# A Trainium2 kernel of two transformer stacks: half of two output chunks ahead of the heads' norm, the fourth chunk ahead of the third, both token blocks scaled in a row

## The reference, cut to what matters

```python
def _retention_diff_mixer(...):        # layer 0
    ret = _merge(_group_norm(_bidirectional_scan(q, k, v, la_f, la_b))) * jax.nn.silu(rg)
    diff = _merge(_rms_norm(o, subln) * (1.0 - lam_init))
    return jnp.concatenate([ret, diff], axis=-1) @ w_out
def _mla_gla_mixer(...):               # layer 1
    gla = _merge(_rms_norm(o, gla_norm)) * jax.nn.silu(gg)
    return jnp.concatenate([mla, gla], axis=-1) @ w_out
# first block, each layer
x = _layer_norm(ALPHA * x + mix, ln1_g[i], ln1_b[i])
x = _layer_norm(ALPHA * x + _hier_moe(x, ...), ln2_g[i], ln2_b[i])   # 32 experts, 2 of them for a token
# second block, each layer: feed-forward, mixer, feed-forward
y_hgrn = head_rms_norm(o, hgrn_norm_g[l]) * jax.nn.silu(g)
mix = jnp.concatenate([y_pool, y_hgrn], axis=-1) @ w_out[l]
x = layer_norm(ALPHA_2 * x + mix, ln_g[l, 1], ln_b[l, 1])
```

## Time and profile before

| | |
|---|---|
| time, median of 3 runs | 2363.29 us (2363.08 to 2366.67) |
| the profiled execution | 2362.22 us, its span 2360.2 us |
| PE busy | 2174.5 us, 92% |
| DVE busy | 1143.2 us, 48% |
| ACT busy | 785.6 us, 33% |
| DMA, mean over the span | 264 GB/s (420 GB/s while the experts run) |
| last products of the mixers' ends | 176.9, 829.0, 1637.9 and 2159.9 us |

### The profile page before, as it was taken

The page is one execution under the profiler, slowest core; times in us unless marked ns, Lnnn a source line. Parts: engine busy times, 40 slices in busy tenths (PEclk is TensorE's granted clock), DMA queues, the critical chain, the costliest instruction groups (busy, mean ns, idle before and its releaser), DMA issues.

```text
span 2360.2 us, 30107 instructions
## 1 busy us (share of the span) xinstructions
PE 2174.5 (92%) x12126; PEld 1535.9 (65%) x12126; DVE 1143.2 (48%) x1782; ACT 785.6 (33%) x1299; POOL 60.4 (3%) x62
## 2 busy tenths in 40 slices
PE   8978998799887889997988999998999999898998
PEld 7874443344367844433433688897888888787887
DVE  5563221121157741211211766676666666776666
ACT  3432110011035321101111455453554555544553
POOL 0010000000010000000000000001000000001000
PEclk9989999899998799999999999999999999999999
DMA  9438999999972289999999855533555555433551
GB/s 292 142 119 360 420 420 421 417 421 421 417 251 72 70 351 420 420 421 415 421 420 420 287 178 202 173 126 114 187 181 197 176 181 198 159 107 125 179 195 56
DMA packets 231542, 622.66 MB, mean 264 GB/s; under 512 B 15456, under 2 KB 166944, under 8 KB 182112
## 3 DMA queue, kind: packets, MB, share of 16 engines
q1 hardware_dynamic: 226096, 605.32, 67.8%
q0 software_dynamic: 3040, 10.78, 1.4%
q10 hardware_dynamic: 2256, 4.50, 0.5%
HBM read 619.51 MB, written 1.05 MB: 263 GB/s over the span
## 4 chain that ended last, share of the span: by engine, by line
PE 41%; DMA 6%; DVE 4%; ACT 2%; issue 1%; SPq 0%; POOL 0%; DVEq 0%; ACTq 0%
PE bank L1507 14%; PE bank L1495 9%; PE bank L1508 7%; PE bank L228 6%; PE bank L1335 3%; DMA arena<-in_moe_w_up 1%; DMA ring<-in_moe_w_up 1%; DMA w_parts<-in_moe_w_up 1%; DMA ring<-in_ffn_gate 1%; DMA x_tok<-in_moe_w_up 1%; DVE w_low L429 1%; PE bank L1663 1%; ACT w_high L422 0%; DVE x_tok L683 0%; DVE x_tok L672 0%
## 5 line engine op out<-in xcount | busy, mean ns | idle before, releaser
L429 DVE TENSOR_TENSOR w_low<-ring,w_high 128x1024 fp32r<-128x1024 f32 x364 | 440.6, 1225 | 270.2 <-ACT w_high L422 270.1
L1507 PE MATMUL bank<-xT_parts,w_high 128*128 128x512 f32 x1408 | 497.8, 396 | 6.0 <-DVE xT_parts L494 6.0
L422 ACT ACTIVATE w_high<-ring 128x1024 fp32r<-128x1024 f32 x364 | 376.9, 1053 | 217.2 <-PE bank L1508 185.6
L1508 PE MATMUL bank<-xT_parts,w_low 128*128 128x256 f32 x1408 | 395.4, 281 | 0.0
L1335 PE MATMUL bank<-ring,arena 128*64 128x512 f32 x1344 | 339.5, 594 | 18.0 <-DMA ring<-in_moe_w_up 5.9
L1507 PEld LDWEIGHTS bank<-xT_parts,w_high 128*128 128x128 f32 x1408 | 264.7, 188 | 69.1 <-DVE xT_parts L494 6.9
L1335 PE MATMUL bank<-w_parts,arena 128*64 128x512 f32 x768 | 262.1, 604 | 12.4 <-DMA w_parts<-in_moe_w_up 5.7
L1508 PEld LDWEIGHTS bank<-xT_parts,w_low 128*128 128x128 f32 x1408 | 266.8, 189 | 3.0
L1335 PEld LDWEIGHTS bank<-ring,arena 128*64 128x64 f32 x1344 | 110.0, 137 | 231.7 <-issue 222.9
L228 PE MATMUL bank<-w_high,xT_parts 128*128 128x256 f32 x1152 | 229.2, 296 | 14.0 <-DVE w_low L429 8.8
L1443 DVE SCALAR_TENSOR_TENSOR arena<-arena,bank 128x512 f32<-128x512 f32 x32 | 23.9, 748 | 435.3 <-PE bank L1335 435.3
(11 more groups left out here) (285 smaller groups left out, 2930.5 us busy)
## 6 DMA issues: line engine op xcount, KB each, us to landing
ring<-in_moe_w_gate SPq DMA_DIRECT2D x56, 1024.0 KB, 24.1
ring<-in_moe_w_up SPq DMA_DIRECT2D x56, 1024.0 KB, 22.1
ring<-in_moe_w_down SPq DMA_DIRECT2D x56, 1024.0 KB, 26.1
ring<-in_ffn_gate SPq DMA_DIRECT2D x44, 1024.0 KB, 6.9
ring<-in_ffn_up SPq DMA_DIRECT2D x44, 1024.0 KB, 5.4
ring<-in_ffn_down SPq DMA_DIRECT2D x44, 1024.0 KB, 6.4
w_parts<-in_moe_w_up SPq DMA_DIRECT2D x32, 1024.0 KB, 26.3
w_parts<-in_moe_w_down SPq DMA_DIRECT2D x32, 1024.0 KB, 26.1
```

Source lines behind the costliest of these rows:

```text
L422: e.activation(hi, src, ACT.Copy).then_inc(*S.high.tell(key))
L429: e.tensor_tensor(lo, src, hi.bitcast(F32), ALU.subtract).then_inc(*S.low.tell(key))
L1507: e.matmul(pairs(bank[:, :]), hi[:, j, :], k.x_parts[:, :, j, :], start=j == 0, stop=False)
L1508: ins = e.matmul(bank[:, 0:T], lo[:, j, :], k.xh[:, j, :], start=False, stop=j == KT - 1)
```

## The change

It does four things, in all four ends:

1. `begin_out_pe` makes the ready half of chunks 0 and 1 (48 products) ahead of the transposes; 144 are left for `out_pe`. Chunk 1 gets a bank for each block.
2. The order of `out_pe` becomes (0,0), (1,0), (0,1), (1,1), (3,0), (2,0), (3,1), (2,1).
3. ScalarE copies the high parts of chunks 1 and 3 before the squares (or, in the even layer, before the mix); VectorE makes chunk 1's low parts ahead of the norm and chunk 3's beside it. What the fourth chunk's copies wait for is now the last reader of that part of the arena (`arena_free`): the last retention scores, the last level's scores, or the last decayed level. In the even layer `b.dq, b.dk, b.rq, b.rk` move to the arena's end.
4. Both blocks are scaled and gated in a row; block 0's mix low part comes after them.

```diff
--- before.py
+++ after.py
@@ -404,6 +404,15 @@
     return src, hi[i][:, :].rearrange("p (a b) -> p a b", a=a), lo[i][:, :].rearrange("p (a b) -> p a b", a=a)
 
 
+def arena_free(k, name, layer):
+
+    if name == "ev_out":
+        return k.S.product, ("ret", 3)
+    if name == "od_out":
+        return k.S.product, k.od.streams[1].last(1)
+    return k.S.dve_step, ("hgrn", layer, 1, "decayed", 1)
+
+
...
     old = k.part_before[key]
     if key[0] in ("ev_out", "od_out", "out2") and key[2] == 3:
-        e.wait_ge(*S.used[key[0:2] + (0, 1)])
+        signal, last = arena_free(k, key[0], key[1])
+        e.wait_ge(*signal[last])
     if old is not None:
         e.wait_ge(*(S.expert[old] if old[0] == "moe" else S.used[old]))
     e.activation(hi, src, ACT.Copy).then_inc(*S.high.tell(key))
@@ -578,48 +588,52 @@
 
 
 
-def begin_out_pe(e, k, name, layer, r, rest):
-
-    S = k.S
-    key = (name, layer, 0)
-    e.wait_ge(*S.low[key + (1,)])
+def begin_out_pe(e, k, name, layer, r, rest, group):
+
+    S = k.S
     for mix in rest:
         e.wait_ge(*S.dve_out[mix])
-    _, hi, lo = split_views(k, key + (r,))
-    for tb in range(NB):
-        bank = k.banks.open(e, B_BANKS, key + ("tb", tb))
-        mm(e, bank[:, 0:256], block_products(k, tb, hi, lo, r * (KT // 2)), last=False)
+    for c in range(2):
+        key = (name, layer, c)
+        e.wait_ge(*S.low[key + (1,)])
+        _, hi, lo = split_views(k, key + (r,))
+        for tb in range(NB):
+            bank = k.banks.open(e, group if c else B_BANKS, key + ("tb", tb))
+            mm(e, bank[:, 0:256], block_products(k, tb, hi, lo, r * (KT // 2)), last=False)
 
 
 def out_pe(e, k, name, layer, r, mixes):
 
     S = k.S
-    for c, tb in ((0, 0), (0, 1), (1, 0), (1, 1), (2, 0), (3, 0), (2, 1), (3, 1)):
+    for tb in range(NB):
+        e.wait_ge(*S.dve_out[mixes[tb]])
+        for c in range(2):
+            key = (name, layer, c)
+            _, hi, lo = split_views(k, key + (1 - r,))
+            ins = mm(e, k.banks[key + ("tb", tb)][:, 0:256], block_products(k, tb, hi, lo, (1 - r) * (KT // 2)), first=False)
+            ins.then_inc(*(S.used.tell(key + (1,)) if tb == 1 else S.product.tell(key + ("tb", 0))))
+    for c, tb in ((3, 0), (2, 0), (3, 1), (2, 1)):
         key = (name, layer, c)
-        if c == 0:
-            bank, c0 = k.banks[key + ("tb", tb)], 0
-        elif c == 1:
-            bank, c0 = k.banks.open(e, A_BANKS, key) if tb == 0 else k.banks[key], tb * 256
-        else:
-            bank, c0 = k.banks.open(e, A_BANKS if c == 2 else B_BANKS, key + ("tb", tb)), 0
+        bank = k.banks.open(e, A_BANKS if c == 2 else B_BANKS, key + ("tb", tb))
         e.wait_ge(*S.low[key + (1,)])
-        e.wait_ge(*S.dve_out[mixes[tb]])
         parts = []
-        for part in (1 - r,) if c == 0 else (0, 1):
+        for part in (0, 1):
             _, hi, lo = split_views(k, key + (part,))
             parts += block_products(k, tb, hi, lo, part * (KT // 2))
-        ins = mm(e, bank[:, c0:c0 + 256], parts, first=c > 0)
-        if tb == 1:
-            ins.then_inc(*S.used.tell(key + (1,)))
-        elif c != 1:
-            ins.then_inc(*S.product.tell(key + ("tb", 0)))
+        ins = mm(e, bank[:, 0:256], parts)
+        ins.then_inc(*(S.used.tell(key + (1,)) if tb == 1 else S.product.tell(key + ("tb", 0))))
+
+
+def out_ahead_act(e, k, name, layer):
+
+    split_chunk(e, k, (name, layer, 1), split_act)
+    split_chunk(e, k, (name, layer, 3), split_act)
 
 
 def out_act(e, k, name, layer):
-    for c in range(4):
-        split_chunk(e, k, following(k, (name, layer, c)), split_act)
-        if c == 2 and name != "out2":
-            split_act(e, k, ("router", 0 if name == "ev_out" else 1))
+    split_chunk(e, k, (name, layer, 2), split_act)
+    if name != "out2":
+        split_act(e, k, ("router", 0 if name == "ev_out" else 1))
 
 
 def residual_dve(e, k, key, blocks, cols, src):
@@ -628,25 +642,18 @@
 
 
 def out_dve(e, k, name, layer, norm):
-    S = k.S
-    for c in range(4):
-        key, cols = (name, layer, c), slice(256 * c, 256 * c + 256)
-        split_chunk(e, k, following(k, key), split_dve)
-        if c == 0:
...
-        if c == 2 and name != "out2":
-            split_dve(e, k, ("router", 0 if name == "ev_out" else 1))
-
-
-def out_last_dve(e, k, name, layer, c, tb):
+    for tb in range(NB):
+        out_residual_dve(e, k, name, layer, 0, tb)
+    split_chunk(e, k, (name, layer, 2), split_dve)
+    for tb in range(NB):
+        out_residual_dve(e, k, name, layer, 1, tb)
+        e.wait_ge(*k.S.dve_out[name, layer, 1, "tb", tb])
+        half_stats(e, k, norm, tb, 0)
+    if name != "out2":
+        split_dve(e, k, ("router", 0 if name == "ev_out" else 1))
+
+
+def out_residual_dve(e, k, name, layer, c, tb):
 
     S = k.S
     key, cols = (name, layer, c), slice(256 * c, 256 * c + 256)
...
@@ -884,7 +891,7 @@
         elif what == "mix":
             for tb in range(NB):
                 mix_transposes_pe(e, k, k.acc[:, :, 512:1024], tb, ("diff_mix", tb), ("diff_o", NB - 1))
-    begin_out_pe(e, k, "ev_out", 0, 1, [("diff_mix", 1)])
+    begin_out_pe(e, k, "ev_out", 0, 1, [("diff_mix", 1)], O_BANKS)
     for tb in range(NB):
         mix_transposes_pe(e, k, k.acc, tb, ("ret_mix", tb), ("ret_y", tb))
     out_pe(e, k, "ev_out", 0, 1, [("ret_mix", 0), ("ret_mix", 1)])
...
+    out_ahead_act(e, k, "ev_out", 0)
     for tb in range(NB):
         mix_write_act(e, k, 0, tb, ("ret_mix", tb))
     out_act(e, k, "ev_out", 0)
...
+    split_chunk(e, k, ("ev_out", 0, 1), split_dve)
     for tb in range(NB):
         part = slice(HEADS * tb, HEADS * tb + HEADS)
         e.wait_ge(*S.product["ret_o", 3])
@@ -1048,8 +1057,7 @@
         ins.then_inc(*S.dve_step.tell(("ret_mean", tb)))
         e.wait_ge(*S.dve_step["ret_mean", tb])
         e.tensor_scalar(k.hrs[:, part], k.hmv[:, part, 1], LN_EPS, None, ALU.add).then_inc(*S.mean_square.tell(("ret", tb)))
-        if tb == 1:
-            mix_write_dve(e, k, 0, 0, ("ret_mix", 0))
+    for tb in range(NB):
         e.wait_ge(*S.root["ret", tb])
         for h in range(HEADS):
             i = tb * HEADS + h
@@ -1059,7 +1067,10 @@
         e.wait_ge(*S.act_out["ret_gate"])
         e.wait_ge(*S.dve_out["ret_o", tb])
         e.tensor_tensor(k.acc[:, tb, 0:512], k.acc[:, tb, 0:512], b.gate[:, tb, :], ALU.mult).then_inc(*S.dve_out.tell(("ret_y", tb)))
+    mix_write_dve(e, k, 0, 0, ("ret_mix", 0))
+    split_dve(e, k, ("ev_out", 0, 3, 0))
     mix_write_dve(e, k, 0, 1, ("ret_mix", 1))
+    split_dve(e, k, ("ev_out", 0, 3, 1))
     out_dve(e, k, "ev_out", 0, norm)
 
 
@@ -1830,13 +1841,14 @@
 
 
 def gated_pe(e, k, name, layer, o_key, rest):
-    begin_out_pe(e, k, name, layer, 0, [rest])
+    begin_out_pe(e, k, name, layer, 0, [rest], A_BANKS)
     for tb in range(NB):
         mix_transposes_pe(e, k, k.acc, tb, o_key + ("mix", tb), o_key + ("gated", tb))
     out_pe(e, k, name, layer, 0, [o_key + ("mix", tb) for tb in range(NB)])
 
 
 def gated_act(e, k, name, layer, o_key):
+    out_ahead_act(e, k, name, layer)
     for tb in range(NB):
         e.wait_ge(*k.S.product[o_key + (tb,)])
         squares_act(e, k, k.banks[o_key + (tb,)], HEADS, HD, k.hrs[:, HEADS * tb:HEADS * tb + HEADS], o_key + (tb,))
@@ -1847,10 +1859,11 @@
 
 def gated_dve(e, k, name, layer, o_key, gain, gate, norm):
     S = k.S
+    split_chunk(e, k, (name, layer, 1), split_dve)
     for tb in range(NB):
         rms_dve(e, k, k.hrs[:, HEADS * tb:HEADS * tb + HEADS], HEADS, HD, o_key + (tb,))
         if tb:
-            mix_write_dve(e, k, 4, 0, o_key + ("mix", 0))
+            split_dve(e, k, (name, layer, 3, 0))
         e.wait_ge(*S.root[o_key + (tb,)])
         for h in range(HEADS):
             ins = e.scalar_tensor_tensor(out=k.acc[:, tb, block(h)], in0=k.banks[o_key + (tb,)][:, block(h)],
@@ -1859,6 +1872,8 @@
         e.wait_ge(*S.act_out[o_key + ("gate",)])
         e.wait_ge(*S.dve_out[o_key + (tb,)])
         e.tensor_tensor(k.acc[:, tb, 0:512], k.acc[:, tb, 0:512], gate[:, tb, :], ALU.mult).then_inc(*S.dve_out.tell(o_key + ("gated", tb)))
+    mix_write_dve(e, k, 4, 0, o_key + ("mix", 0))
+    split_dve(e, k, (name, layer, 3, 1))
     mix_write_dve(e, k, 4, 1, o_key + ("mix", 1))
     out_dve(e, k, name, layer, norm)
 
@@ -2703,15 +2718,15 @@
 
 def norm_after_mixer_dve(e, k, name, layer, n):
     S = k.S
-    out_last_dve(e, k, name, layer, 2, 0)
-    out_last_dve(e, k, name, layer, 3, 0)
-    e.wait_ge(*S.dve_out[name, layer, 3, "tb", 0])
+    out_residual_dve(e, k, name, layer, 3, 0)
+    out_residual_dve(e, k, name, layer, 2, 0)
+    e.wait_ge(*S.dve_out[name, layer, 2, "tb", 0])
     half_stats(e, k, n, 0, 1)
     norm_centre_dve(e, k, n, 0)
-    out_last_dve(e, k, name, layer, 2, 1)
+    out_residual_dve(e, k, name, layer, 3, 1)
     norm_scale_dve(e, k, n, 0)
-    out_last_dve(e, k, name, layer, 3, 1)
-    e.wait_ge(*S.dve_out[name, layer, 3, "tb", 1])
+    out_residual_dve(e, k, name, layer, 2, 1)
```

(22 more changed lines are left out.)

## The result

The changed kernel takes 2344.39 us (median; 2341.41 to 2348.00) against 2363.24 us: ratio 0.9918, 95% interval 0.9904 to 0.9932, some 19.4 us faster. The forecast was 2348.3 us, 3.9 us too much. The measured time lies inside the stated range of 2341.5 to 2354, but just under the forecast's own part of it, 2345 to 2351: between the forecast and rival A's 2342.1. The profiled execution took 2341.99 us, its span is 2339.9 us.

What follows compares the result with a forecast made beforehand. TensorE's chain at the four mixer ends was taken as the bound, also starting the DMA-bound experts. Gains 7.9 + 5.4 + 0.4 + 1.3 = 15.0 us from 2362.2 gave 2347.2; the median's 1.1 made 2348.3 us, range 2341.5 to 2354.

Steps and rivals of the forecast that it cites:

- rival A: Better: root not held (2.2 us) and upper clock at both `out2` restarts (about 4 us), 2342.1 us; chance 0.16.
- rival C: Swallowed: the experts' DMA stream starts no earlier, 13.3 us of the first two ends lost, 2361.6 us; chance 0.10.
- The moved products: All four ends: 24 products go ahead of the transposes, leaving 144 behind the restart instead of 168; 2.9 us an end.
- The fourth chunk ahead: All four ends: TensorE's 1.54 us wait for the fourth chunk's low parts goes; 1.5 us gained, 0.2 us to spare.
- Even restart: Even end: blocks scaled in a row let products restart at about 151.25, 1.5 us earlier.
- Clock at the even and odd restart: With idle time near 1 us TensorE restarts at the upper clock, gaining 2.0 us (even) and 1.4 us (odd).
- rival B: Weaker: TensorE stays at half speed at the even and odd restarts too (3.4 us), 2351.7 us; chance 0.17.
- Root held: Odd and both `out2` ends: GpSimd's second root is held by VectorE's low part beside it, 0.8 us later.
- `out2` restarts: Four copies ahead of the squares and the held root make the second scaling 4.0 and 3.1 us later.
- `out2` clock: Both `out2` restarts: idle stretches no less than before in the first, so half speed stays and no gain was counted.
- The experts' stream: Experts' DMA stream is started by TensorE's chain, so an earlier start gives an earlier end, one for one.
- Rivals C and D: C: stream starts no earlier, 2361.6 us, chance 0.10; D: ScalarE held at fourth chunk's copies, 2369 us, chance 0.03.

Runs made afterwards that it cites:

- unmoved: Changed kernel with chunk 1's ready half computed behind the restart again, copies and low parts left in place: ratio 0.9989 to the kernel before.
- before_fill: Kernel before the change, with unread filler products ahead of the second block's transposes, eight at the even end and six at the odd: ratio 1.0014.
- root_free: Changed kernel with chunk 3's low parts moved behind the mix's in three ends, so none runs beside the second root: ratio 0.9925 to the kernel before.
- fill_out2: Changed kernel with seven unread filler products between the two blocks' transposes in both `out2` ends: ratio 0.9933 to the kernel before.
- third_first: Changed kernel with the third chunk's products and residuals ahead of the fourth's again, copies and low parts left in place: ratio 0.9985 to the kernel before.
- apart: Changed kernel with block 0's mix low part ahead of the second scaling again and the fourth chunk's low parts behind both scalings: ratio 0.9957 to the kernel before.
- row_only: Kernel before the change, with only both blocks scaled in a row and block 0's mix low part behind them: ratio 0.9972.

## Why the prediction was right, and where its sizes were off

All four ends gained more than was forecast, 4.1 us in all by the ledger, so no two errors had to cancel. (A slip in the chances has no consequence: "the same" got 0.09 where rival C alone has 0.10.)

**The moved products** (2.9 an end): right. unmoved gives 3.0 to 5.4 us back; 2.9 of it is the products' own time.

**The fourth chunk ahead** (1.5 an end): right; no such wait is left behind the restart. The third chunk is just in time: 0.6 us to spare at the even end and 0.4 in the others, where 0.2 was reckoned.

**Even restart** (1.5 earlier): t2 came 2.1 earlier. The statistics began on VectorE 0.3 us sooner than reckoned and took 1.42 us a block, not 1.5. The odd restart (0.45 later) came 0.1 later by t2.

**Clock at the even and odd restart** (2.0 and 1.4): behind t2 the even end took 6.7 us less where 2.9 + 1.5 + 2.0 = 6.4 was the sum, the odd one 6.0 where it was 5.8. The sizes are right, and rival B is out: both restarts run at 1.00. But they hang on something that the prediction didn't name, chunk 1's early parts: before_fill shows that alone these terms are worth 1.1 and 0.1.

**Root held** (0.8 in three ends): 0.90, as root_free shows by taking it away. By the Trainium skill, "SBUF — State Buffer", section "SBUF: two separate sides", the port pair that the two engines share is an exclusive lock, taken also by a VectorE operation with two SBUF inputs against a GpSimd operation that reads SBUF. The trace agrees: 1.91 us beside the low part, 1.01 without it.

**`out2` restarts** (4.0 and 3.1 later): 3.85 and 2.98. Right.

**`out2` clock** ("I leave the half speed as it was"): this is the term that was mis-sized. With 18.12 us for transposes and 144 products at the upper level (the even end), the lower level costs 24.77 - 18.12 - 2.9 - 1.53 = 2.2 us in the first `out2` end before and 19.26 - 18.12 = 1.1 after; 2.4 and 1.1 in the second. (With fill_out2's 17.70 in place of 18.12 each is 0.4 more, the differences are the same.) That is 1.1 and 1.3 us unforecast, 2.4 of the 4.1 us by which the sum of the ends exceeds 15.0. Rival A had about 4 us for it, and somewhat over half came true; its other part, a root that isn't held, did not. The runs don't show what sets the length of the slow stretch.

**After the last product**: right. `out2`'s last residual of block 1 follows the last product by 0.2 us as before, with the feed-forward's low parts ahead of it.

**The experts' stream**: right. It starts at 195.37 instead of 205.22 (2.6 us of that had come ahead of the even end). From the last product to that load it was 1.5 us longer in this profile, in which the gather ran at half speed, and the stream to the odd end is as long as before. Rivals C and D are out: the first by that earlier load and a time that fell as much as the ends did, the second by copies that had no wait, but for 0.61 us at the odd end, where ScalarE is early anyway.

What the sum didn't say is that its parts depend on each other. Alone they shorten the ends by 8.8, 2.1 and -5.3 us, 5.6 together; all three in one kernel give 19.1. Undone one by one, by the edits above, they cost 16.0, 7.6 and 15.7. The moved products make the transposes late, which needs the blocks in a row; they also shorten the time that the third chunk has, which needs the fourth ahead of it; and they need chunk 1's parts early, which is what lets the faster restart count.

## What to carry to other kernels

Where several edits meet on one chain, price each with the others in place, and ask what the chain waits for next once the one is there: a part that costs the ends 5 us alone can be the largest gain in company. Measure a stage from a point of its own just ahead of it: here the same unedited lines put the start of the even end at 133.9 to 136.2 us in eight executions and at 131.1 to 131.9 in six others. Work that is only "ahead" still has an order: the same copies woven between the squares instead of in front of them, with the low parts behind them, were worth 7 to 9.5 us more.

## What the runs showed of the hardware that wasn't expected

A wait of 2.5 us in the middle of dense products cost 4.1 to 4.7 us in third_first, since TensorE then ran at its lower level for a part of the next 4 us; a wait of 2.26 us at that run's even end cost 2.5, and the clock stayed up. The length of the idle time alone doesn't decide it. In apart the even end has these second transposes, and this window behind them:

```profile
155.20 0.63 PE L730 MATMUL bank<-tables,acc 128*128 128x128 f32 x4 [3.58 <-DVE acc L1070]
```
```profile
155.20:157.00 1.80, 1.80 (x16) 1.80 (x17) 1.49 (x2) 0.60 (x1) 0.00 (x0) 1.00 0.01 5
```

After 3.58 us without work it stayed at 1.00, while the same program's odd end, after 3.33 us, ran at 0.54. In row_only the even end stayed at 1.00 behind 1.50 and 1.45 us, while unmoved fell to 0.50 at its even end behind 1.90 and 1.44 us:

```profile
154.00:156.00 2.00, 2.00 (x12) 2.00 (x11) 1.59 (x3) 0.00 (x0) 0.00 (x0) 0.50 0.00 0
```

And the same lines at 68 to 76 us were granted 1.00 in six of the profiled executions and 0.50 to 0.57 in the other eight. What tells these apart the runs don't show.
